# Prompt attention with scores and maxima contracted over 64 rows in two halves of the array, and pair sums on POOL

## What is computed

```
c = jnp.cumsum(log_f, axis=1)
s = jnp.einsum('bqhd,bkhd->bhqk', q, k).astype(jnp.float32) * (HEAD_DIM ** -0.5)
s = s + jnp.swapaxes(c_q, 1, 2)[..., :, None] - jnp.swapaxes(c_k, 1, 2)[..., None, :]
causal = jnp.arange(k.shape[1])[None, :] <= q_pos[:, None]
s = jnp.where(causal, s, -jnp.inf)
p = jax.nn.softmax(s, axis=-1)
return jnp.einsum('bhqk,bkhd->bqhd', p.astype(v.dtype), v)
```

## Time and profile before

| | us |
|---|---|
| median of 3 runs | 3519.77 (3518.38 to 3529.66) |
| the profiled execution | 3541.94 |
| its span in the trace | 3540.4 |
| prologue of the prompt attention (1104.5 to 1152.2) | 47.7 |
| its six heads (1152.2 to 2507.9) | 248.8, 226.5, 225.2, 225.2, 223.2, 206.8 |

### The profile page before, as it was taken

One profiled execution on the slowest core, in us unless ns is written; L12 is line 12 of the kernel. 1 busy time (PEld: TensorE's weight loads), 2 busy tenths in 40 slices (PEclk: granted clock), 3 DMA queues, 4 the chain that ended last, 5 costly groups with the idle time before them and its releaser, 6 DMA issues. The chain is left out here.

```text
span 3540.4 us, 46435 instructions
## 1 busy us (share of the span) xinstructions
PE 3208.9 (91%) x14828; PEld 2114.3 (60%) x14828; DVE 1976.8 (56%) x3161; ACT 965.7 (27%) x1840; POOL 891.7 (25%) x1615
## 2 busy tenths in 40 slices
PE   7999999999995999999999999999676895499998
PEld 6888888888773444444444444444243552277776
DVE  5434434434223787877868778687277565334342
ACT  2111111111111344444444444444233111022120
POOL 3475766757733667000000000000000000000000
PEclk9999999999996799999999999999877787699999
DMA  6545545554423323001001010000211775334432
GB/s 191 176 146 185 195 146 176 187 184 149 153 90 82 85 58 85 25 20 43 19 24 38 23 39 25 22 23 5 69 57 62 198 220 148 122 102 154 142 104 78
DMA packets 322887, 358.70 MB, mean 101 GB/s; under 512 B 152620, under 2 KB 253716, under 8 KB 322652
## 3 DMA queue, kind: packets, MB, share of 16 engines
q1 hardware_dynamic: 250068, 244.43, 23.3%
q10 hardware_dynamic: 61872, 74.09, 6.1%
q0 software_dynamic: 10720, 37.31, 3.1%
HBM read 256.04 MB, written 99.61 MB: 100 GB/s over the span
## 5 line engine op out<-in xcount | busy, mean ns | idle before, releaser
L1285 ACT ACTIVATE p<-bank,ncol 128x512 f32<-128x512 f32 (+1 forms) x864 | 541.6, 654 | 744.7 <-PE bank L1424 530.8
L1155 DVE TENSOR_REDUCE pm<-bank 128x1 f32<-128x512 f32 (+2 forms) x864 | 528.5, 642 | 209.0 <-PE bank L1355 146.5
L1375 PE MATMUL bank<-p,v_tok 128*64 128x512 f32 (+2 forms) x1728 | 419.8, 591 | 0.6 <-ACT o_parts L1266 0.5
L677 PE MATMUL bank<-xhi,whi 128*128 128x512 f32 x1024 | 410.3, 401 | 8.5 <-issue 7.9
L677 PE MATMUL bank<-xhi,wlo 128*128 128x512 f32 x1024 | 404.7, 395 | 0.0
L677 PE MATMUL bank<-xlo,whi 128*128 128x512 f32 x1024 | 403.9, 394 | 0.0
L1423 PE MATMUL bank<-qhi,kst 128*128 128x512 f32 (+1 forms) x864 | 383.4, 444 | 13.6 <-ACT p L1285 7.4
L1355 PE MATMUL bank<-kone,qone 66*128 66x512 f32 (+2 forms) x864 | 343.2, 418 | 35.5 <-DVE pm L1155 17.7
L1424 PE MATMUL bank<-qlo,kone 66*128 66x512 f32 (+1 forms) x864 | 335.7, 389 | 0.0
L571 DVE CAST whi<-wraw 128x3072 fp32r<-128x3072 f32 (+2 forms) x64 | 107.6, 1681 | 367.1 <-PE bank L677 271.4
L1190 DVE TENSOR_TENSOR p_pairs<-p 128x512 f32<-128x512 f32 (+2 forms) x432 | 278.0, 676 | 44.6 <-PE bank L1395 39.9
(11 more groups left out here) (398 smaller groups left out, 4998.7 us busy)
## 6 DMA issues: line engine op xcount, KB each, us to landing
wraw<-in_w_in SPq DMA_DIRECT2D x40, 1536.0 KB, 7.0
x_tok<-in_x_prompt SPq DMA_DIRECT2D x32, 512.0 KB, 5.6
wraw<-in_w_in SPq DMA_DIRECT2D x16, 1024.0 KB, 5.9
gate_t<-fstage ACTq DMA_DIRECT2D x64, 256.0 KB, 2.5
mx_x<-in_x_prompt SPq DMA_DIRECT2D x32, 512.0 KB, 3.2
out_y_prompt<-mx_xo ACTq DMA_DIRECT2D x32, 512.0 KB, 2.7
wraw<-in_w_in SPq DMA_DIRECT2D x8, 1560.0 KB, 8.4
ssm_consts<-st_part POOLq DMA_DIRECT2D x12, 1024.0 KB, 5.2
```

What stands on the lines that cost most here:

```text
L677: mm = pe.matmul(dst, lhsT, rhs, start=(k == 0 and ws is whi and xs is xhi), stop=(k == KD - 1 and ws is wlo))
L1155: dve.tensor_reduce(pm[:, b % 2, r, ch:ch + 1], c.bank[XB + n % NPRE][:, 0:w], AX.X, ALU.max).then_inc(pre_max, 1)
L1285: act.activation(p[:, n % PS, q0:512], c.bank[score_bank[n]][:, q0:512], ACT.Exp, bias=ncol[:, KG * r + i:KG * r + i + 1]).then_inc(ex, 1)
L1375: pe.matmul(c.bank[OB][rows, q0:512], v[:, KG * r + i, :], p[:, (n0 + i) % PS, q0:512], start=(r == 0 and q0 == 0), stop=(r == b and i >= ...
```

## The change

**Scores.** All operands have 64 rows. Two key tiles lie beside each other in `kst`, one in rows 0 to 63 and one in rows 64 to 127, and their products (L1468 of the changed kernel) go to two banks, each in its own half of the array: three products a tile (high by high, low keys by high queries, high keys by low queries). The row of maxima is a product of its own with a contraction over one row (L1460), the four tiles of a step in four groups of 32 rows and in banks 0 to 3. The masks are two products of 64 by 64 a tile (L1429).

**First pass.** It uses the same halves (L1443): a pair of products for key tiles in the two halves, banks 4 and 5, the only two. There are 80 such pairs a head, with 156 tiles. The gate sums of the keys are no longer in the product: DVE adds them from a table of 128 rows and takes the maximum in one instruction (`tensor_tensor_reduce`, L1251). The pass runs 11 steps ahead; in each step the first pair comes before the scores and the rest after them, and 27 pairs of the first head fall into the prologue.

**Around it.** The pair sums move from DVE to POOL (L1183, L1185), between the items of the cached past, of which one follows each step (two in the first and last head). Folds, key turns and rows of maxima use banks 4 and 5 as well; ACT copies the fold out (`copy_folded`), and DVE divides from SBUF. The keys' tables are doubled and used by turns of two heads.

The core of the diff:

```
-    pre = [(b, r, ch, 512 if ch < b else (r + 1) * P) for b in range(NB) for r in range(4) for ch in range(b + 1)]
+    pre = [(b, r, g, (min(GT, 4 * b + r + 1 - GT * g) + 1) // 2, min(GT, 4 * b + r + 1 - GT * g) // 2)
+           for b in range(NB) for g in range(b // 2 + 1) for r in range(4)]
...
+    AHEAD = 11
+    cost = [sum(64 + P * n for n in x[3:] if n) for x in pre]
+    first_at = [NST * (2 * sum(cost[:n]) + cost[n]) // (2 * sum(cost)) - AHEAD for n in range(len(pre))]
...
+            def masked(bank, x, t0, mask, mm):
+                rows = slice(HD * x, HD * (x + 1))
+                for half in range(2):
+                    mm = pe.matmul(bank[HD * half:HD * (half + 1), t0:t0 + P], c.identb[rows, rows], mask[rows, half, :],
+                                   start=False, stop=True, skip_group_check=True, tile_position=(HD * x, HD * half))
+                return mm
...
+            def first_pass(h, par, n):
+                for kind, x_, e in uses_of(n):
+                    rows = slice(HD * e, HD * (e + 1))
+                    w = P * pre[n][3 + e]
+                    diagonal = g == b // 2 and e == r % 2
+                    mm = pe.matmul(c.bank[XB[e]][:, 0:w], qhi[rows, b, q], kst[rows, par, 0, 512 * g:512 * g + w],
+                                   start=True, stop=not diagonal, skip_group_check=True)
+                    if diagonal:
+                        mm = masked(c.bank[XB[e]], e, w - P, mqk, mm)
...
-                        pe.matmul(bank[:, q0:512], kst[:, j * P:(j + 1) * P], qhi[:, b % QS, q0:512], start=True, stop=False)
-                        mm = pe.matmul(bank[:, q0:512], kone[:, j * P:(j + 1) * P], qlo[:, b % QS, q0:512], start=False, stop=True)
+                for i in range(KG):
+                    x = 32 * (2 * (i % 2) + i // 2)
+                    pe.wait_ge(ex, num(at(NMN, h, KG * st + i - KG + 1)))
+                    pe.matmul(c.bank[i][:, q_from(st, i):512], one4[x:x + 1, :], mq[x:x + 1, b % MS, q_from(st, i):512],
+                              start=True, stop=False, skip_group_check=True, tile_position=(x, 0))
+                for i0 in (0, 2):
+                    for khl_, q_ in ((0, qhi), (1, qhi), (0, qlo)):
+                        for i in (i0, i0 + 1):
+                            rows = slice(HD * (i % 2), HD * (i % 2 + 1))
...
-                    dve.tensor_reduce(pm[:, b % 2, r, ch:ch + 1], c.bank[XB + n % NPRE][:, 0:w], AX.X, ALU.max
+                    dve.tensor_tensor_reduce(junk[:, x % 2, 0:w], c.bank[XB[e]][:, 0:w], ncb[:, e, 512 * g:512 * g + w], 1.0, NEG,
+                                             ALU.add, ALU.max, pm[:, b % 2, r, 2 * g + e:2 * g + e + 1]).then_inc(pre_max, 1)
...
-                    dve.tensor_tensor(out[:, q1:512], p[:, n % PS, q1:512], p[:, (n + 1) % PS, q1:512], ALU.add).then_inc(paired, 1)
+                    pool.tensor_tensor(out[:, q1:512], p[:, n % PS, q1:512], p[:, (n + 1) % PS, q1:512], ALU.add).then_inc(paired, 1)
...
+            def copy_folded(h, b):
+                act.wait_ge(folded, num(NB * h + b + 1))
+                act.wait_ge(o_norm, num(at(NB, h, b)))
+                act.activation(fsb[:], c.bank[XB[1]][:], ACT.Copy).then_inc(f_copied, 1)
```

More of the change, by code:

```diff
@@ L894, in q_from @@
         return i * P if r == b else 0
[L897 to L908, removed]
@@ L911, in cuts @@
[L911 to L921, removed]
@@ new lines, in body @@
+            def body(h, par, is_first, last):
+                at_ends = is_first or last
+                work = past.work(nc, pool, a, c, past_k[:], past_q[:], (0 if is_first else 6 if last else num(h + 1)), 2 if at_ends else 1)
+                for st in range(NST):
+                    pairs(h, st)
+                    for _ in range(2 if at_ends else 1):
+                        next(work, None)
+                for _ in work:
+                    pass
+            past.begin(nc, pool, a)
@@ L1246, in _ @@
+            split_q(0, 0)
+            for g in range(1, NKG):
+                split_k(0, g)
+                split_q(0, g)
+            columns(0, 0)
+            for b in range(NB):
+                if b >= NKG and Q_SPLIT[b] < 0:
+                    split_q(0, b)
+                for n in range(pre_end[b - 1] if b else 0, pre_end[b]):
+                    if first_at[n] < 0:
+                        maxima(0, n)
+                if row_at[b] < 0:
+                    row(0, b)
             heads(dve, body)
-            pairs(NF, -1)
@@ new lines, in body @@
+            def body(h, par, is_first, last):
+                place = 0 if is_first else 2 if last else 1
+                for st in range(NST):
+                    early, late = pairs_at(st)
+                    for found in (early, late):
+                        for n, dh in found:
+                            if runs(h, dh, is_first, last):
+                                for kind, x_, e in uses_of(n):
+                                    bank_free(h, place, kind, dh, x_)
+                                first_pass(h + dh, par if dh == 0 else 1 - par, n)
+                        if found is early:
+                            scores(h, par, st)
@@ L1764, in load @@
                 pool.dma_start(k_buf[:, ch % 2, n % CP, :], ck[page]).then_inc(self.k_in[ch % 2], 16)
-        def body(b, last):
+        for b in (b0 + j for j in range(count)):
+            if not (isinstance(b, int) and b == 0):
+                pool.wait_ge(self.summed, PER * NCK * b)
+                pool.sem_inc(self.turn, 1)
+            pool.dma_start(q_buf, c_q[b].partition_broadcast(P)).then_inc(self.q_in, 16)
+            yield
+            load(b, 0)
+            yield
+            load(b, 1)
+            yield
             for ch in range(NCK):
```

738 lines of the change are left out of this document (380 added, 358 removed).

## The result

The changed kernel takes 3665.04 us (median of 4 runs, 3659.03 to 3669.04) against 3519.78: the ratio is 1.0412, 95% interval 1.0397 to 1.0428. The forecast was 3578. The direction is as forecast, and 3665 lies in the whole range of 3440 to 3680, but the loss is 145 us where 58 were forecast, and 3665 is over the 3535 to 3650 that the prediction gave to the account it ranked first.

A forecast was written before the change was run, and what follows sets the result against it. PE was taken to bound each head. Products -20.5, shape changes +26 and waits +3 give +8.5 us a middle head; four +34, first head -11, last +5, prologue +30, together +58: 3578 us, range 3440 to 3680.

The forecast's parts named there:

- the account it ranked first: Whole kernel: the summed terms hold, giving 3578 us, own range 3535 to 3650, chance 0.52.
- Who sets the end: Prompt attention heads: PE sets the end of a head, other engines only where PE waits for them.
- Term 1: Scores and first pass on PE: products side by side in halves stream 88 fewer widths, -20.5 us a head.
- rival E: Products on PE: halves don't overlap with one bank each, 56 us more a head, some 3900 us; chance 0.03.
- Term 2: PE around rows of maxima and masks: 170 more changes of array shape at 0.15 us, +26 us a head.
- rival B: Changes between row groups on PE are cheap, 0.05 us each: 3476 us, or 3410 with fewer waits; chance 0.30.
- Term 3: PE's waits in the heads, mainly for first-pass banks: 21 us in place of 18, +3 us net a middle head.
- rival C: Six heads: waits in each step lower PE's clock from 0.97 to 0.90, +98 us, 3676 us; chance 0.06.
- The prologue: Before the heads: 27 first-pass pairs run one by one at half clock, 52 us in all, +30 us.
- The first head: First head, 248.8 us: becomes a middle head with some half clock at its start, 238 us, -11 us.
- POOL at nothing: Pair sums on POOL: two a step at 1.33 us each plus a past item are covered, costing nothing.
- rival D: POOL becomes the bound if a pair sum takes 1.9 us or more: 3620 us or more; chance 0.03.

The follow-up runs named there:

- e1: Changed kernel with each mask as two accumulating products of 64 rows by 128 columns in its half of the array: 3608.73 us.
- e3: Changed kernel with both masks and rows of maxima as products in halves of the array: 3584.54 us.
- e9: Changed kernel with each maximum taken over only the last 128 keys of its bank, leaving out part of the first pass: 3607.39 us.
- e13: Changed kernel with one edit, a block's fold written to bank 7 in place of bank 5: 3630.92 us.
- e6: Changed kernel with the prologue's first-pass pairs in three pairs of banks by turns in place of one: 3649.66 us.
- the second profile: The kernel before, unchanged, run and profiled again: 3520.40 us, and 3517.1 us in its profile.
- e7: Changed kernel with the pair sums back on DVE, POOL keeping only the cached past: 3702.64 us.
- e4: Changed kernel with first-pass pairs spread over the steps by number in place of by columns: 3698.98 us.
- e5: Changed kernel with the third and later first-pass pairs of a step moved behind the sums: 3670.04 us.
- e12: e11 with a least cost of 600 for narrow pairs and the first pass 10 steps ahead in place of 11: 3543.53 us.
- e2: Changed kernel with each row of maxima added by a 64-row product in one half of the array: 3659.12 us.
- e11: Changed kernel with masks and rows of maxima in halves, three prologue bank pairs, first query loads earlier, and the fold in bank 7: 3523.39 us.

## Why the prediction was right or wrong

By stretch, the four middle heads were forecast +34 us and measured +90, the prologue +30 and +46, the first head -11 and +10, the last +5 and +1.

**Who sets the end: right.** PE is the busiest engine of every head after, as before; DVE is busy 130 of 244 us, ACT 101, POOL 112. But PE stands idle 25 of the 244, most of them waiting for DVE and ACT.

**Term 1, the products: right.** Four scores in 0.46 us show the halves side by side; rival E is out. The eight records of the earlier trace rows that the prediction calls products are four products of two records each; its sum is the same.

**Term 2, changes of shape: right in kind, near in size.** In this loop a change around the rows of maxima costs 0.20 us (0.43 and 0.44 less 0.233), and one around a mask 0.11 by e1, where 0.15 was taken for both; 72 of the one and 98 of the other are 25 us a head, where 26 were forecast. e1 and e3 show that the changes cost by themselves: without them, with more streaming in their place, the kernel is 80 us faster. The Trainium skill (TensorEngine Tiling (Array Packing), Tiling Modes, Key Properties) says that a change of the tiling mode drains the engine; these runs agree with it and add the price. Terms 1 and 2 forecast +5.5 us a middle head, and PE's work measured +1.3, or +5 if the 3.6 us of small waits that the prediction estimates are taken out of the work before. So rival B, cheap changes, is refuted as it was put: the work saved by the halves and the work added by the changes about cancel. The 3.07 times for four 32-row tiles, which the prediction took from the Trainium skill (TensorE: Matmul & The Clock Gate, Part 3, Measured speedup vs the span model), stays untested: the 0.87 us from the first-pass pair to the first score hold two changes as well, and no run parts them.

**Term 3, the waits: the step that failed.** It was put as 21 us in place of 18, +3 a middle head. Measured, in six heads, are 87 us more idle and 21 more lost to the clock, 108 in all, 18 a head; in the four middle heads it is 21 a head, 34 in place of 13. Its parts:

- *The waits of before were taken too high.* The profile used was a long one; in the second one a head from the third to the fifth has 7 us of idle and 3 to 4 of clock loss, 11 and not 14, with the small waits beside.
- *The single pair of banks.* Forecast were 8 for the further pairs and 3 for the division, measured 13.4 a middle head for the maxima (13 or 14 waits in place of 10). The price per pair was made of DVE's instructions alone. The turn of a bank also has the product, the way to DVE and the way back: 1.1 us at half clock in the prologue, with long maxima and with short ones (e9), and halving DVE's part took off only a third of the wait.
- *The fold and its like.* Forecast were 4 and 3, measured 5.6 for ACT's copy of the fold and 4.5 for key turns and rows. e13 gives the fold's bank 34 us in all.
- *Half clock.* Forecast was 3 a middle head, measured 9 (mean of the four, from 4 to 17).

Against the +3 forecast, the +21 measured are 7 us more of idle, 6 more of clock, and 5 less on the side of before, where the 3.6 us of small waits do not show as idle but stand in the work. The measured 3665 lies near the 3676 of rival C, but not by its mechanism: C put 98 us on the clock, and the clock took 21 more.

**The prologue: right in kind, too small.** Forecast +30, measured +46. A full pair took 2.41 us (2.3 forecast), but a diagonal one 1.3 to 3.1, 2.3 on the mean and not 1.7, and the turn of each block's maxima was left out of the sum (0.8 us three times, and 2.0 at the fourth, with a wait for queries): 67.7 us of first pass where 52 were forecast. The first pair started at 1131, 11 us after before's, behind all key turns and the loads of queries; against that, before's prologue had 11 us behind its first pass, and the changed one has none. e6 shows the bank part, 26 us.

**The first head: wrong sign.** Forecast -11, measured +10 against the second profile and -5 against the first, from which it was worked out. So 15 of the 21 are the long first head of that profile. DVE's busy time did fall, from 194 to 128 us, but PE's idle rose from 13 to 25.

**POOL at nothing: right.** An add took 1300 ns, with 1330 forecast, and PE never waits for POOL in its list of waits, so rival D is out. e7 shows that the move is worth 38 us, which the forecast did not see: it took DVE's work as covered, while it stands in the chain of the maxima.

**Left open.** What makes the clock fall where it does. Heads with the same instructions got 0.98 and 0.93, e6's shorter prologue was followed by a head that took 8 us more at a lower clock, and e9, with a third of the waits for maxima gone, kept all of the loss. No run here holds the clock fixed, and it moved by up to 34 us with edits that left PE's products alone (e4, e5, e12), so a saving in waits can't be foretold to better than that.

## What to carry to other kernels

When a change packs products tighter but gives them fewer banks, count for each bank the whole turn (product, way to the reader, reader, way back) and who else is queued for it; the streaming saved can come back as waits (in e2, 26 us less work made the kernel 6 us faster). Keep a run of products in one shape of the array even if some then stream more columns: masks in halves were 56 us faster here, and rows of maxima in halves, two widths a step in place of one, another 24. And try an edit again once its neighbour's wait is gone: the third pair's move gave nothing on the changed kernel and 34 us on e11, where the fold had a bank of its own and the masks and rows their one shape. Read idle, clock and work apart for each run, since an edit that cuts one can raise another. Profile the kernel before twice.

## What the runs showed that was not expected

The adds on POOL stretch some of DVE's instructions with two operands in SBUF: the split of the queries (L1228) took 934 ns on the mean with the pair sums on POOL and 752 with them on DVE (e7), the split of the keys (L1219) 811 and 696, the gating (L1279) 511 and 433; the product of the division (L1272), also with both operands in SBUF, did not get longer (425 and 458). The maxima, with one operand in a bank, stay at 688 ns for 512 columns in both, plus 83 for the read-out. By group, the changed kernel, columns as in the earlier trace rows:

```profile
L1251 DVE CUSTOM_DVE_ANT_0 first_junk<-bank,negc_all 128x512 bf16<-128x512 f32 x648 | 422.6, 688 | 436.2 <-PE bank L1443 392.4 <-PE bank L1429 43.4 <-issue 0.2
L1251 DVE DVE_READ_ACCUMULATOR2_ANT pm<- 128x1 f32 x936 | 78.0, 83 | 0.0
```

And two profiles of one kernel can differ by 15 us in one head of 240.
